# Tile work in turns behind the norms of two FFNs, and half-width matmuls side by side, in a two-block transformer kernel on one core

## The reference

```python
# layer 0: convolution and gated mixing, then a SwiGLU FFN
x = x + m2 * mixer(modulate(rmsnorm(x), m0, m1)); x = x + m5 * (silu(h @ w1) * (h @ w3)) @ w2
# layer 1: latent attention with 8 heads, then 8 experts of which 2 are taken
z = h @ w_in                      # q_lat 384, kv_lat 256, k_pe 64
k = [rmsnorm(kv_lat) @ w_ukv (128 per head), rope(k_pe) (64, shared by all heads)]
q = rmsnorm(q_lat) @ w_uq         # per head 128 plain + 64 rotated columns
x = x + m2 * softmax(q @ k.T * scale) @ v @ w_o ; x = x + m5 * moe(h)
# second block: window attention, state space, block attention; heads of 64, 2 key heads each
x = x + (g1 * ya + g2 * yb + g3 * yc) @ w_out
x = x + relu(rmsnorm(x) @ w_ff1)**2 @ w_ff2 ; out = rmsnorm(x)
```

## Time and profile before

| | |
|---|---|
| median of 3 runs | 2534.75 us (2533.33 to 2537.76) |
| profiled execution, its own time | 2546.07 us |
| its span, first to last instruction | 2544.3 us |
| PE busy | 2373.6 us, 93% of the span |
| DVE, ACT busy | 1703.8 us, 1316.7 us |
| mean granted clock of TensorE | 0.972 |

### The profile page before, as it was taken

The page is one execution under the profiler, slowest core; times in us unless marked ns, Lnnn a source line. Parts: engine busy times, 40 slices in busy tenths (PEclk is TensorE's granted clock), DMA queues, the critical chain, the costliest instruction groups (busy, mean ns, idle before and its releaser), DMA issues.

```text
span 2544.3 us, 32252 instructions
## 1 busy us (share of the span) xinstructions
PE 2373.6 (93%) x11484; PEld 1851.7 (73%) x11484; DVE 1703.8 (67%) x2365; ACT 1316.7 (52%) x1802; POOL 56.8 (2%) x93
## 2 busy tenths in 40 slices
PE   6999899999799799989999999999999899998998
PEld 3557688887346687668766888887666587877997
DVE  4895432345323598989888989898898647724554
ACT  3124322244213387868787878777778424312443
POOL 0000000000310000000000000000000300000000
PEclk8999899999889899999999999999999999999999
DMA  9873233222120399989899989899999432233541
GB/s 385 337 308 111 87 100 99 91 91 79 37 99 1 128 349 343 371 331 363 333 371 346 372 331 363 338 359 348 368 359 370 177 115 84 100 120 145 180 184 50
DMA packets 183885, 580.24 MB, mean 228 GB/s; under 512 B 4688, under 2 KB 29392, under 8 KB 177104
## 3 DMA queue, kind: packets, MB, share of 16 engines
q1 hardware_dynamic: 183616, 578.11, 61.0%
q0 software_dynamic: 144, 0.52, 0.1%
HBM read 577.57 MB, written 1.05 MB: 227 GB/s over the span
## 4 chain that ended last, share of the span: by engine, by line
PE 67%; DVE 13%; DMA 8%; issue 5%; ACT 3%; DVEq 3%; ACTq 0%; SPq 0%
PE psum L771 16%; PE psum L778 14%; PE psum L779 14%; PE psum L780 14%; DMA ring<-in_o_exp_w 8%; DVE region_r L2276 5%; DVE region L1950 2%; ACT region_r L1632 2%; DVEq L1953 2%; PE psum L794 1%; PE psum L1116 1%; PE psum L1107 1%; PE psum L1108 1%; PE psum L1017 1%; PE psum L1016 1%
## 5 line engine op out<-in xcount | busy, mean ns | idle before, releaser
L2276 DVE TENSOR_TENSOR region_r<-ring,region_r 128x1024 fp32r<-128x1024 f32 x756 | 898.1, 1220 | 98.3 <-ACT region_r L1632 78.9
L1632 ACT ACTIVATE region_r<-ring 128x1024 fp32r<-128x1024 f32 x756 | 782.7, 1057 | 235.8 <-PE psum L780 151.1
L778 PE MATMUL psum<-region_r 128*128 128x512 f32 (+1 forms) x2072 | 767.9, 371 | 46.7 <-DVE region_r L2276 13.1
L779 PE MATMUL psum<-region_r 128*128 128x512 f32 (+1 forms) x1976 | 719.4, 364 | 0.0
L780 PE MATMUL psum<-region_r 128*128 128x512 f32 (+1 forms) x1976 | 719.4, 364 | 0.0
L778 PEld LDWEIGHTS psum<-region_r 128*128 128x128 f32 x2072 | 394.8, 191 | 126.8 <-issue 39.5
L780 PEld LDWEIGHTS psum<-region_r 128*128 128x128 f32 x1976 | 376.1, 190 | 59.1
L779 PEld LDWEIGHTS psum<-region_r 128*128 128x128 f32 x1976 | 376.5, 191 | 56.3
L1107 PE MATMUL psum<-region_r 128*128 128x512 f32 x672 | 289.7, 431 | 39.1 <-DVE region_r L2276 38.5
L1108 PE MATMUL psum<-region_r 128*128 128x512 f32 x672 | 265.3, 395 | 0.0
L1107 PEld LDWEIGHTS psum<-region_r 128*128 128x128 f32 x672 | 126.6, 188 | 137.5 <-DVE region_r L2276 114.9
(11 more groups left out here) (344 smaller groups left out, 2111.8 us busy)
## 6 DMA issues: line engine op xcount, KB each, us to landing
ring<-in_o_exp_w SPq DMA_DIRECT2D x189, 2048.0 KB, 9.3
ring<-in_w_ada SPq DMA_DIRECT2D x24, 2048.0 KB, 11.3
ring<-in_w_ff SPq DMA_DIRECT2D x16, 2048.0 KB, 8.8
ring<-in_e_ffn_w SPq DMA_DIRECT2D x22, 1024.0 KB, 7.9
ring<-in_w_in SPq DMA_DIRECT2D x10, 2048.0 KB, 8.5
region<-in_e_w_in SPq DMA_DIRECT2D x4, 2048.0 KB, 15.0
ring<-in_e_ffn_w SPq DMA_DIRECT2D x4, 2048.0 KB, 7.7
ring<-in_e_w_out SPq DMA_DIRECT2D x2, 2048.0 KB, 9.0
```

What stands on the lines that cost most here:

```text
L778: pe.matmul(out, a_hi, b_hi, start=first, stop=False)
L779: pe.matmul(out, a_hi, b_lo, start=False, stop=False)
L1632: act.activation(w_hi[:, q % SPLIT, :], ring[:, expert_slot(j), r * QUARTER:(r + 1) * QUARTER], ACT.Copy).then_inc(s_split_hi, 1)
L2276: dve.tensor_tensor(w_lo[:, q % SPLIT, :], ring[:, expert_slot(j), r * QUARTER:(r + 1) * QUARTER], w_hi[:, q % SPLIT, :].bitcast(F32), ALU ...
```

## The change

1. **Norms of two FFNs.** DVE scales tile k and then makes the low part of tile k - 1 (`behind`), so the low parts come in turns with the scalings. The third and fourth weight units of the first FFN are split before the tiles on ACT and between them on DVE; in the last FFN the first unit is split already while the layer before ends, and the second between the tiles.
2. **Square root's table early.** `norm` on ACT takes the root of a constant (`warm`) ahead of the squares of four norms, which moves the table load there.
3. **Half width in pairs.** Matmuls with 64 output columns go alternately into partitions 0 to 63 and 64 to 127: the "dup" projections; the rotated columns of q, where the halves are two heads; and k_pe, which is now projected into both halves (16 matmuls in place of 8). cos, sin and rot are loaded into both halves of the partitions, and DVE works on 128 partitions: two blocks of three operations in place of four. `rot` takes four matmuls, each pair on disjoint halves.
4. **Scores of two heads in pairs.** Units are ordered so that two heads stand side by side; PE makes the plain scores of both, then the rotated ones, whose contractions lie on partitions 0 to 63 and 64 to 127. Four banks hold scores in place of three.

```diff
@@ loads
-            sp.dma_start(const[:, :], A["const"]).then_inc(s_small_in, 16)
+            own = CONST_COLS["rot"][0]
+            sp.dma_start(const[:, 0:own], A["const"][:, 0:own]).then_inc(s_small_in, 16)
+            for half in range(2):
+                sp.dma_start(const[64 * half:64 * half + 64, own:], A["const"][0:64, own:]).then_inc(s_small_in, 16)
@@ PE, k_pe
-            group(bank2(2)[0:64], [(slot(n, KT, 320)[:, k, 256:320], H[:, :, k, :]) for k in range(KT)]
-                  ).then_inc(s_lat_ready, 1)
+            for k in range(KT):
+                for rows in (slice(0, 64), slice(64, P)):
+                    mm = pe.matmul(bank2(2)[rows], slot(n, KT, 320)[:, k, 256:320], H[:, :, k, :], start=(k == 0), stop=(k == KT - 1))
+            mm.then_inc(s_lat_ready, 1)
@@ PE, q of two heads
+                for half in range(2):
+                    group(bank(b + half)[:, 0:T], [(w[:, k, c + 192 * half:c + 192 * half + P], q_lat[:, 0, k, :]) for k in range(3)])
+                for k in range(3):
+                    for half in range(2):
+                        at = c + 192 * half + P
+                        mm = pe.matmul(bank(b)[64 * half:64 * half + 64, T:2 * T], w[:, k, at:at + ROPE], q_lat[:, 0, k, :],
+                                       start=(k == 0), stop=(k == 2))
@@ PE, attention
+            for u in range(0, UNITS + 4, 2):
                 if u < UNITS:
+                    for v in (u, u + 1):
+                        h, q0 = mla_unit(v)
+                        pe.matmul(bank2(S_BANKS[v % 4]), q_n[:, h, q0:q0 + P], k_n[:, h, :, :], start=True, stop=False)
+                    for v in (u, u + 1):
+                        h, q0 = mla_unit(v)
+                        rows = slice(64 * (h % 2), 64 * (h % 2) + 64)
+                        mm = pe.matmul(bank2(S_BANKS[v % 4]), q_r[rows, h // 2, q0:q0 + P], k_pe[rows, :, :], start=False, stop=True)
+                    mm.then_inc(s_s_ready, 2)
+                for v in (u - 2, u - 1):
...
@@ PE, keys of the second block
-                    for half in range(2):
-                        mm = group(b[64 * half:64 * half + 64, 0:T], [(w[:, k, c:c + HEAD], H[:, 0, k, :]) for k in range(KT)],
-                                   None if t or half else N_MIX2)
+                    for k in range(KT):
+                        if t == 0:
+                            pe.wait_ge(s_h_ready, tiles_before(N_MIX2) + k + 1)
+                        for half in range(2):
+                            mm = pe.matmul(b[64 * half:64 * half + 64, 0:T], w[:, k, c:c + HEAD], H[:, 0, k, :],
+                                           start=(k == 0), stop=(k == KT - 1))
@@ ACT, norm
+                if n in FOLDED:
+                    act.activation(warm[:, :], ones[:, 0:1], ACT.Sqrt)
@@ DVE, behind the last norm
+            def ff_tile_lo(k):
                 dve.wait_ge(s_n_hi_ready, k + 1)
                 dve.tensor_tensor(n_lo[:, k, :], H[:, 0, k, :], n_hi[:, k, :].bitcast(F32), ALU.subtract).then_inc(s_n_lo_ready, 1)
+                if k == 2:
+                    ff1_lo(0, 0, 1)
+
+            norm(N_FFN2, X, H, column("norm_ffn"), s_h_ready, ff_tile_lo)
```

More of the change, by code:

```diff
@@ L44, with mla_unit @@
 SSM_TILES = 16
+UNITS = 2 * MLA_HEADS
+S_BANKS = (0, 1, 2, 7)
+def mla_unit(u):
+    return 2 * (u // 4) + u % 2, P * (u // 2 % 2)
 SSM_L = 128
@@ L963, in _ @@
             pe.wait_ge(s_lat_sb, 6)
-            pe.matmul(psum[0:64, 2, 0:T], cn("rot")[0:64, :], k_pe[0:64, 0, :], start=True, stop=True).then_inc(s_rot_ready, 1)
+            for rows in (slice(0, 64), slice(64, P)):
+                mm = pe.matmul(psum[rows, 2, 0:T], cn("rot")[rows, :], k_pe[rows, 0, :], start=True, stop=True)
+            mm.then_inc(s_rot_ready, 1)
             n = CH_UKV
@@ L994, in _ @@
                 w = slot(n, 3, 768)
[L995 to L999, removed]
-                pe.wait_ge(s_q_sb, 2 * i + 2)
[L1001 to L1006, removed]
@@ new lines, in _ @@
+                mm.then_inc(s_q_ready, 1)
+            for i in range(2):
+                pe.wait_ge(s_q_sb, 2 * i + 2)
+                pe.wait_ge(s_v_sb, 8)
+                for rows in (slice(0, 64), slice(64, P)):
+                    mm = pe.matmul(psum[rows, 4 + i, :].rearrange("p (h t) -> p h t", h=2), cn("rot")[rows, :],
+                                   q_r[rows, 2 * i:2 * i + 2, :], start=True, stop=True)
+                mm.then_inc(s_rot_ready, 1)
+            pe.wait_ge(s_q_sb, 4)
@@ L1544, in ffn_up @@
             def ffn_up(c, cs):
-                for u in range(0 if cs else 2, 8):
+                for u in range(0 if cs else 4, 8):
                     ffn_hi(c, cs, u)
@@ L1587, in _ @@
                 act.activation(k_n[:, h, :, :], bank2(h % 4), ACT.Copy).then_inc(s_kn_sb, 1)
[L1588 to L1592 removed]
+            for j in range(MLA_HEADS // 2):
+                act.wait_ge(s_q_ready, j + 1)
+                b = 2 * (j % 2)
+                for half in range(2):
+                    act.activation(q_n[:, 2 * j + half, :], bank(b + half)[:, 0:T], ACT.Copy)
+                act.activation(q_r[:, j, :], bank(b)[:, T:2 * T], ACT.Copy).then_inc(s_q_sb, 1)
             for u in range(UNITS + 3):
@@ L1774, in ff1 @@
             def ff1(c, cs):
-                for u in range(0 if cs else 1, 4):
+                for u in range(0 if cs else 2, 4):
                     ff1_hi(c, cs, u)
@@ L1806, in _, with norm @@
         def _(dve):
-            def norm(n, src, dst, g, signal):
+            def norm(n, src, dst, g, signal, behind=None):
                 kt, sets, _ = NORMS[n]
@@ L1818, in norm @@
                     i.then_inc(signal, 1)
+                    if behind and k:
+                        behind(k - 1)
+                if behind:
+                    behind(kt - 1)
             def fold_squares(n, squares, k):
@@ L2037, in _, with ffn_tile_lo @@
             ffn_lo(0, 0, 1)
-            modulated(N_FFN0)
-            for k in range(KT):
+            def ffn_tile_lo(k):
                 dve.wait_ge(s_ffn_h_hi, k + 1)
```

138 lines of the change are left out of this document (66 added, 72 removed).

## The result

The changed kernel takes 2507.88 us (median of 4 runs, 2505.80 to 2513.79), the kernel before 2536.26 (4 runs). The medians lie 28.4 us apart. The ratio is 0.9875, 95% interval 0.9853 to 0.9898; of 2536.26 that is 31.7 us less, with 25.9 to 37.3 inside the interval. The forecast was 2502 and 32.8 us less, the range 2494 to 2514.

What follows compares the result with a forecast made beforehand. PE was taken as the bound, busy 2373.6 of 2544.3 us. Terms 3.3 + 0 + 6.5 + 4.0 + 6.8 + 4.5 + 4.4 + 3.3 + 0 = 32.8 gave 2513.3 profiled, 2502 median; range 2494 to 2514.

Steps and rivals of the forecast that it cites:

- First norm: First FFN's norm: PE starts 3.7 us earlier, of which 3.3 stay because the third unit needs DVE's sixth low tile.
- q: Rotated columns of q: two heads take 4.23 us in place of 5.86, 6.5 us gained over four pairs.
- Attention: Block attention: a pair of units takes 6.26 us against 6.79, one pair at low clock; gain 6.8, bounds 3.7 and 10.
- rival 2: Ahead of the attention the clock does not fall: attention takes 52.5 us, 3.2 less, total 2498.8; chance 0.15.
- Window keys: Doubled keys ka0 and ka1, in pairs, end at 2018.9 in place of 2023.4: 4.5 us gained.
- block keys: Doubled keys of the block attention: 3.5 us each in place of 6.31; gains 1.7 and 2.75, sum 4.4.
- Last norm: Last FFN's norm: table load 1.3 us earlier and low parts in turns with scalings; 3.3 us kept (2.6 to 4).
- Start: Program start: two more transfer instructions ahead of X on SP's queue give back 0.3 us, up to 0.9.
- Rival 1: Rot's contraction halves, writing one bank, run one after the other: 0.86 us later, total 2502.9; chance 0.12.
- Rival 3: Attention's order eats the pairs: each of eight waits another 0.85 us, attention keeps 62.6, total 2509; chance 0.12.
- 4: Halves do not overlap with 64 output columns: only 2.9 us gained, total 2531.9; chance 0.02.
- 5: Halves neither overlap nor change freely: 120 half-width matmuls at 0.1 us each cost 12, total 2543.9; chance 0.03.

Runs made afterwards that it cites:

- dup_apart: The changed kernel with the four doubled key projections again done one half after the other: 2513.66 us, ratio 0.9906 to the kernel before.
- kpe_apart: The changed kernel with the 16 half-width k_pe matmuls as eight on one half, then eight on the other: 2512.37 us, ratio 0.9902 to the kernel before.
- q_apart: The changed kernel with the rotated columns of q's two heads as three matmuls on one half, then three on the other: 2501.91 us, one execution.
- late_tables: The changed kernel without the early square roots of a constant, so the table load stands behind the squares again at four norms: 2519.68 us, one execution.
- scores_apart: The changed kernel with PE making plain and rotated scores of one unit, then of the next: 2527.72 us, ratio 0.9953 to the kernel before.
- fill: The changed kernel with unused matmuls of ones by ones at six places where PE idled: 2496.91 us, ratio 0.9834 to the kernel before.

## Why the prediction held, point by point

The mechanism, halves of PE that overlap in turns, is shown by `dup_apart`, `kpe_apart` and `q_apart`, and the sum was 32.8 against 31.7 measured. That it came so close is in part luck: the attention gave 2.9 more than its term, and the first norm, k_pe's stage, the start and a longer low clock in the second block gave less. By its terms:

- *First norm* 3.3, measured 2.7. PE starts 3.7 earlier as forecast. The reason given for the loss, DVE's sixth low tile, is wrong: no row waits there. PE's clock stayed low until about 270 us, as in the kernel before, so the earlier start buys low-clock steps: 13 matmuls went at 0.50 (the window 264.5 to 270.0 above), where before nine did.
- *k_pe* 0. The group takes 7.0, as before and as forecast. The stage is 0.5 longer ahead of it: PE's first 4.3 us there went at the low clock, and 3.1 before.
- *q* 6.5, measured 6.5 (4.24 a pair). Its reading as pure overlap of turns was in part right: half after half already overlaps at the handover, as `q_apart` shows. The rows of before held this too, since 32 instructions of 0.216 would be 6.9 and a doubled key took 6.3.
- *Rotation* 4.0, measured 9.17 - 5.29 = 3.9.
- *Attention* 6.8, measured 9.7: the largest error. The pass of 6.26 and its waits were right to 0.01; the low stretch was some 3.4 us long, not a whole pair, and cost 1.6 (52.9 - 51.3) where 3.2 were put down; the ends of the loop were laid out 1.2 too long. The result is close to rival 2's 52.5, but not by rival 2's reason: the clock did fall.
- *Window keys* 4.5, measured 5.2; *block keys* 4.4, measured 1.7 + 2.6. At the first of them PE now waits 0.88 for L2476, as foreseen. These are 9.5, and the stage shows 7.2: behind the last turning the clock was low for 10 us in this trace and for 7 before, which is 1.7 of the difference.
- *Last norm* 3.3, of which the last stage shows 3.5 less; but the 1.3 was put down to the table alone, and the weight copy that the change also moved accounts for it as well (`late_tables`).
- *Start* -0.3, measured -1.0 at N_FFN0 and 0.2 to 1.9 at the first sum over the traces: at the edge of the allowance of 0.9.

Rival 1 is out: L1025's eight instructions of both row halves, in one bank, lie in 2.18 us, and one after the other they would need 8 x 0.43 = 3.4. The Trainium skill, "TensorEngine Tiling (Array Packing)", Gotcha 1: PSUM Pressure, would have had them apart; with the halves on disjoint partitions of the bank the trace disagrees. The Trainium skill, "TensorEngine Tiling (Array Packing)", Tiling Modes, says that a change of tiling mode drains TensorE. With that the trace agrees as far as the cost goes: in scores_apart the four scores of a pass, with three changes of depth among them and one behind, take 4.12 and not 4 x 0.86 = 3.44, which is 0.17 a change. Rival 3 is out by the pass of 6.26, 4 and 5 by kpe_apart and dup_apart.

## What to carry to other kernels

Matmuls that leave half of the array unused are worth pairing, but only turns at the finest grain get all of it; half after half already gets back about four instructions' time per handover. When one queue's order shows up as a wait, look at what every other engine has queued for the same place before moving it: here DVE's order alone gave nothing and both gave 5 us. A wait on PE costs itself and then the low clock behind it; independent matmuls in the wait bring the second part back, if they stand behind every signal PE owes and end before the data come. They kept the clock at 1.00 in the six places of `fill` and saved time in five, and they did not keep it ahead of the router, where it fell in the thin matmuls that followed.

## What the runs showed that I had not expected

- Twelve filling matmuls (2.9 us) took 8.6 us off one attention. The low stretch behind 3.1 us of idle time was 3.4 us in one kernel and 20 us in one that differs only in the order of the scores, one trace each; behind the last turning of the second block the same matmuls had 3 to 10 us.
- The experts' stage, unchanged, took between 1149.7 and 1164.0 us in thirteen traces. That is nearly half of the effect studied here, and stage marks are the way around it.
- A half that follows the other half in the same bank's other partitions starts before the first one's last matmuls end, worth 0.8 us with 256 columns and 1.7 with 512: about four instructions.
